# States of a diagonal state-space layer stored by planes of the step index, stepped for all pairs at once, with three early pieces of the gated projection

## The reference

```python
u = (h @ w_in)
lam_bar = jnp.exp(lam * dt)                       # 64 groups x 64 complex states
b_bar = ((lam_bar - 1.0) / lam)[..., None] * b_c
bu = einsum(u, b_bar)                             # 16 inputs of a group -> 64 states
xs[t] = lam_bar * xs[t-1] + bu[t]
y = real(einsum(xs, c_c)) + d_skip * u
g = gelu(y)
val, gate = split(g @ w_glu, 2)
x = x + val * sigmoid(gate)
```

## Time and profile before

| | us |
|---|---|
| median of three runs (lowest, highest) | 950.24 (949.27, 950.56) |
| the profiled execution: its time | 950.29 |
| its span | 948.5 |
| PE busy | 736.2 |
| DVE busy | 302.0 |
| ACT busy | 186.5 |
| POOL busy | 75.1 |

### The profile page before, as it was taken

The page is one execution under the profiler, slowest core; times in us unless marked ns, Lnnn a source line. Parts: engine busy times, 40 slices in busy tenths (PEclk is TensorE's granted clock), DMA queues, the critical chain, the costliest instruction groups (busy, mean ns, idle before and its releaser), DMA issues.

```text
span 948.5 us, 15405 instructions
## 1 busy us (share of the span) xinstructions
PE 736.2 (78%) x6273; PEld 432.3 (46%) x6273; DVE 302.0 (32%) x702; ACT 186.5 (20%) x398; POOL 75.1 (8%) x64
## 2 busy tenths in 40 slices
PE   2969485994697668676699996666398999996696
PEld 1859354432554334343344444333354555553453
DVE  5792997115421001100421533223711111211112
ACT  3653430123110000000300324113210111110012
POOL 6691000002100000000000000001200000000000
PEclk9986797995699888878899997877599999999899
DMA  9520502934399999999990472016089990499991
GB/s 262 148 96 1 179 1 75 419 130 197 103 425 425 424 424 423 424 424 423 390 338 1 178 266 89 0 41 247 1 352 423 420 402 0 158 422 424 422 418 63
DMA packets 58074, 238.40 MB, mean 251 GB/s; under 512 B 17624, under 2 KB 17824, under 8 KB 33440
## 3 DMA queue, kind: packets, MB, share of 16 engines
q1 hardware_dynamic: 56560, 235.25, 62.2%
q0 software_dynamic: 576, 2.10, 0.6%
q10 hardware_dynamic: 880, 0.23, 0.1%
HBM read 236.53 MB, written 1.05 MB: 250 GB/s over the span
## 4 chain that ended last, share of the span: by engine, by line
PE 49%; DVE 19%; SPq 16%; DMA 10%; ACT 3%; issue 2%; ACTq 0%; DVEq 0%
SPq L369 16%; PE ps L1573 9%; PE ps L1504 9%; DMA work<-in_moe_w_down 6%; PE ps L1539 5%; PE ps L1439 4%; PE ps L1486 4%; PE ps L1546 4%; DMA ring<-in_moe_w_down 3%; PE ps L1638 3%; PE ps L1360 1%; PE ps L1295 1%; PE ps L1468 1%; DVE work L961 1%; DVE work L962 1%
## 5 line engine op out<-in xcount | busy, mean ns | idle before, releaser
L1504 PE MATMUL ps<-ring,work 128*32 128x256 f32 x1824 | 148.5, 421 | 34.9 <-DMA ring<-in_moe_w_up 24.0
L1504 PEld LDWEIGHTS ps<-ring,work 128*32 128x32 f32 x1824 | 79.9, 121 | 79.9 <-issue 54.9
L1154 DVE TENSOR_TENSOR work<-ps,work 128x256 f32<-128x256 f32 x21 | 12.9, 616 | 300.4 <-PE ps L1504 300.4
L1504 PE MATMUL ps<-work 128*32 128x256 f32 x864 | 87.1, 425 | 27.5 <-DMA ring<-in_moe_w_up 10.8
L1546 PE MATMUL ps<-work 128*128 128x512 f32 x168 | 77.7, 605 | 0.0
L1486 PE MATMUL ps<-work,hT 128*128 128x128 bf16 x736 | 71.2, 227 | 6.7 <-DVE work L1104 6.7
L1504 PEld LDWEIGHTS ps<-work 128*32 128x32 f32 x864 | 45.5, 122 | 62.7 <-issue 44.3
L1573 PE MATMUL ps<-ring,hT 128*128 128x512 f32 x160 | 70.4, 593 | 0.0
L1539 PE MATMUL ps<-ring,work 128*32 128x512 f32 x496 | 65.5, 595 | 6.1 <-DMA work<-in_moe_w_down 4.4
L1486 PE MATMUL ps<-work 128*128 128x128 bf16 x368 | 68.3, 227 | 0.0
L1486 PEld LDWEIGHTS ps<-work,hT 128*128 128x128 bf16 x736 | 59.6, 102 | 15.8 <-issue 8.6
(11 more groups left out here) (288 smaller groups left out, 990.0 us busy)
## 6 DMA issues: line engine op xcount, KB each, us to landing
ring<-in_moe_w_gate SPq DMA_DIRECT2D x24, 2048.0 KB, 25.3
ring<-in_moe_w_down SPq DMA_DIRECT2D x23, 2048.0 KB, 15.4
ring<-in_moe_w_up SPq DMA_DIRECT2D x17, 2048.0 KB, 23.1
work<-in_moe_w_up SPq DMA_DIRECT2D x15, 2048.0 KB, 22.9
work<-in_moe_w_down SPq DMA_DIRECT2D x9, 2048.0 KB, 27.6
work<-in_moe_w_gate SPq DMA_DIRECT2D x8, 2048.0 KB, 25.9
ring<-in_attn_w_qkv SPq DMA_DIRECT2D x5, 2048.0 KB, 21.2
ring<-in_ssm_w_glu SPq DMA_DIRECT2D x4, 2048.0 KB, 8.8
```

Of the source, the lines that this page charges most:

```text
L1154: TTo(hid.rearrange("s (k p) -> s p k", k=2), ps[:, 7, 0:256].rearrange("s (p k) -> s p k", k=2), sil.rearrange("s (p k) -> s p k", k=2), ...
L1504: ins = mm(ps[s, 6 + j // 2, 0:256], xg[:, k, s], pairs[slots[e // 2]][:, e % 2, k, :], start=(k == 0), stop=(k == KD - 1))
```

## The change

1. `X` is laid out by planes of the step: per partition `i`, `l`, `r`, `h`, with `h` innermost and `r` next. `U4` and `gT` follow the same order of the blocks.
2. `local_states` and `carries` run once for all 32 pairs instead of twice for 16. `skips(0)` and `skips(1)` stand inside `local_states`, after steps 4 and 6.
3. `carried(o)` no longer puts its last sum into `X` but into a copy `Xs[o]` in the order that `y` reads, split by `i`; two small copies bring the plane `l` = 0.
4. `weights(2)`, `weights(3)` and `stack` stand ahead of `powers(mu, ...)`. After the powers DVE keeps the increments of octets 0 and 1 (`inputs_kept`); ACT keeps those of octets 2 and 3 only.
5. PE: `drive(2)` stands ahead of `turn_w1(3, 1)`, and `taps(0)`, `taps(1)` ahead of `drive(3)`. The taps use PSUM banks 6 and 7, and `local_states` waits for the last of octet 3.
6. PE: `glu(2, range(4))` is a third piece ahead of `y(2)`. The outputs come in the order 0, 2, 1, 3.
7. Start: DVE clears a third of what POOL cleared of `W2`, POOL clears the rest only after the normalised input is written, and the exponential on ACT no longer waits for the load of `ssm_d`.
8. SP: the first two expert units wait for `y_done` instead of `state`, the next pair but one for the third GLU output.

```diff
-        X = part(12288, 64 * M).rearrange("p (i r m) -> p i r m", i=2, r=PAIRS)
+        X = part(12288, 64 * M).rearrange("p (i l r h) -> p i l r h", i=2, l=SEG, r=PAIRS)
...
+        GLU_OUT = (4, 6, 0, 4)
+        GLU_ORDER = (0, 2, 1, 3)
...
+        def inputs_kept(copy, o, b):
+
+            src = ps[:, 2 * (o % 2) + b, :].rearrange("p (r i l h) -> p i l r h", r=4, i=2, l=SEG)
+            pr = slice(OCT * o + 4 * b, OCT * o + 4 * b + 4)
+            for i in range(2):
+                copy(X[:, i, 0, pr, 1:SEG], src[:, i, SEG - 1, :, 0:SEG - 1])
+                ins = copy(X[:, i, 1:SEG, pr, :], src[:, i, 0:SEG - 1, :, :])
+            return ins
...
-            clear(part(4096, 8192), 8)
+            pool.wait_ge(normed, 2)
+            clear(part(8192, 4096), 4)
...
-            act.wait_ge(s_lam, 64)
+            act.wait_ge(s_lam, 48)
...
+                    n = SEG if l < SEG - 1 else SEG - 1
+                    dst = X[:, :, l + 1, :, :] if l < SEG - 1 else X[:, :, 0, :, 1:SEG]
+                    by = lambda i: spread(spread(mu[:, i, 0, :], 1, 2), 3, n)
+                    advance(dst, X[:, :, l, :, 0:n], tmp[0][:, :, :, 0:n], tmp[1][:, :, :, 0:n], by)
+                    if l in (4, 6):
+                        skips(l // 2 - 2)
...
+                for i in range(2):
+                    dve.tensor_copy(Xs[o][:, i, :, 0:SEG], X[:, i, 0, pr, :])
+                link(TTo(dst, dst, tmp[0].rearrange("p i l r h -> p i l (r h)"), ALU.add))
+                for i in range(2):
+                    ins = TTo(Xs[o][:, i, :, SEG:64].rearrange("p r (l h) -> p l r h", h=SEG), X[:, i, 1:SEG, pr, :], tmp[1][:, i], ALU.add)
...
-                act.copy(gT[:, 2 * o:2 * o + 2, :].rearrange("p c (m s) -> p c s m", s=SB),
-                         ps[:, o, :].rearrange("p (s c m) -> p c s m", s=SB, c=2)).then_inc(g_ready, 1)
+                for c in range(2):
+                    ins = act.copy(gT[:, 2 * o + c, :].rearrange("p (h l s) -> p s l h", h=SEG, s=SB),
+                                   ps[:, o, :].rearrange("p (s c l h) -> p c s l h", s=SB, c=2, l=SEG)[:, c])
```

More of the change, by code:

```diff
@@ L176, in build @@
         Cb = pre[:, 8192:10240].rearrange("p (i r c) -> p i r c", i=2, r=PAIRS)
+        Xs = [pre[:, 6144 + 1024 * n:7168 + 1024 * n].rearrange("p (i r m) -> p i r m", i=2, r=OCT) for n in range(PAIRS // OCT)]
         t1 = pre[:, 10240:10752]
@@ L387, in _ @@
             sp.wait_ge(w2_ready, 4)
-            sp.wait_ge(state, 4)
+            sp.wait_ge(y_done, 4)
             whole(0, 0, 0)
@@ L673, in _ @@
             keep_g(3)
[L675 to L679, removed]
+            for turn_no, n in enumerate(GLU_ORDER):
+                act.wait_ge(glu_done, turn_no + 1)
+                if turn_no >= 1:
+                    act.wait_ge(mixed, turn_no)
+                act.activation(sig[:, 0, :], ps[:, GLU_OUT[n] + 1, :], ACT.Sigmoid).then_inc(sig_ready, 1)
             def moe(l):
@@ L832, in _ @@
             dve.sem_inc(hid_ready, 1)
+            for k in range(4):
+                ins = dve.memset(part(4096 + 1024 * k, 1024), 0.0)
+            ins.then_inc(half_clear, 1)
             L = lambda n: lam[:, n, :]
@@ L944, in _ @@
             weights(1)
+            weights(2)
+            weights(3)
+            dve.wait_ge(u_done, 8)
+            for n in range(8):
+                stack(dve.tensor_copy, 3, n).then_inc(u4_ready, 1)
             link(dve.tensor_copy(mu[:, 0:2, 0, :], Pw[:, 0:2, 4, :]))
@@ L949, in _ @@
             link(TS(mu[:, 2, :, :], mu[:, 1, :, :], -1.0, None, ALU.mult))
[L950 to L954, removed]
+            for o in range(2):
+                for b in range(2):
+                    dve.wait_ge(v_done, 2 * o + b + 1)
+                    link(inputs_kept(dve.tensor_copy, o, b))
+                    dve.sem_inc(v_kept_x, 1)
             def advance(dst, src, P_, Q_, by):
@@ L962, in advance, with skips @@
                 link(TTo(dst, dst, Q_, ALU.add))
[L964 to L969, removed]
+            def skips(half):
+                dve.wait_ge(k_done, 2 * half + 2)
+                taps = ps[:, 6 + half, :].rearrange("p (q n) -> p q n", q=KD // 2)[:, :, 0:PC]
+                TTo(taps, taps, skip[:, 4 * half:4 * half + 4, :], ALU.add).then_inc(k_ready, 1)
@@ L1397, in _ @@
             turn_w1(3, 0)
+            drive(2)
             turn_w1(3, 1)
-            drive(2)
+            taps(0)
+            taps(1)
             drive(3)
-            for o in range(4):
-                taps(o)
+            taps(2)
+            taps(3)
             def y(o):
```

108 lines of the change are left out of this document (50 added, 58 removed).

## The result

The changed kernel takes 938.39 us (median of 4 runs, 935.32 to 940.88) against 949.75 for the kernel before in the same comparison (949.13 to 950.56): a ratio of 0.9878, 95% interval 0.9845 to 0.9912. Repeated with five rounds it is 939.01 against 948.73, 0.9889 (0.9875 to 0.9904).

The account below looks back on a forecast made before the run. The end of the state-space layer was taken to bound the rest, with PE the bound from `state` 1. With start, input stage and states summed, the GLU's end moved from 207.7 to 202.6: 950.29 - 5.1 = 945.1 us, range 939.5 to 950.5.

Parts of the forecast that it names:

- (d): Output stage: PE is the bound from `state` 1; the last GLU product's end moves from 207.7 to 202.6, -5.1 us.
- third piece: Third early GLU piece ahead of `y(2)`: alone worth nothing, it only moves 6.9 us of PE work.
- (a): Start: the root of the norm moves from 13.60 to about 11.7, -1.9 us for all that follows.
- (b): Input stage: powers behind stacking, drives 0 and 1 take 7.3 us instead of 13.9; states start at 91.5 against 89.91.
- rival A: Input stage: the clock does not fall before `drive(2)`; 5.5 us less, 939.6 us; chance 0.18.
- (c): States: 2.83 us a step, DVE in all 45.9 us against 70; `state` 4 at 137.4, where it was 160.
- Rival C: States: operands repeated along the innermost axis keep 2 ns; 7.8 us on `state` 1, hence 952.9 us; chance 0.12.
- Behind the GLU: Rest of the span behind the state-space layer: a shift of that layer's end moves it one to one.

Follow-up runs that it names:

- third piece undone: Changed kernel with the third early GLU piece put back behind `y(2)` and `y(3)`: 938.29 us, ratio 0.9895 to the kernel before.
- order alone: Kernel before with one edit, DVE's powers moved behind `weights(2)`, `weights(3)` and the stacking: 941.89 us, ratio 0.9882.
- filler: Changed kernel plus three products of 512 columns, result unread, between `turn_w1(3, 0)` and `drive(2)`: 940.32 us, ratio 0.9916 to the kernel before.
- late halves: Changed kernel, states in two halves of 16 pairs, the first still waiting until all octets are kept: 933.3 us, ratio 0.9821 to the kernel before.
- powers first: Changed kernel with DVE's powers back between `weights(1)` and `weights(2)`: 950.0 us, ratio 1.0015 to the kernel before.
- early halves: Changed kernel, states in two halves of 16 pairs, the first starting once DVE has kept octets 0 and 1: 915.14 us, ratio 0.9646 to the kernel before.

## Why the prediction fell short

**The step that failed** is the pricing of PE's work by its pace in one launch. The sum took stretches as they had run in one launch of the kernel before, partly at half clock, and carried them to places where PE comes from other work. In (d) `y(2)` and `y(3)` stood at 9.4 us and took 8.0 in each launch below. The first product of the input stage, whose pace had no term at all, was left at its 5.85 us and took 3.69 to 5.27; 29 matmuls of `y(0)` were taken at 5.49 and took 4.48 to 5.66; and the stretch behind the GLU was taken to keep its length, but was up to 2.9 us shorter. Nearly all of these errors have one sign. The forecast against three profiled launches, of which the third differs only in the place of the third piece (us):

| | forecast | changed kernel | repeated run | third piece undone |
|---|---|---|---|---|
| first product of the input stage | 5.85 | 3.69 | 5.27 | 3.69 |
| first drive | 61.6 | 59.55 | 60.51 | 59.16 |
| states start | 91.5 | 84.48 | 90.11 | 88.45 |
| first GLU product | 135.2 | 127.02 | 133.63 | 130.58 |
| last GLU product ends | 202.6 | 193.0 | 199.6 | 196.5 |
| rest of the span | 740.8 | 740.5 | 737.9 | 740.0 |
| span | 943.3 | 933.5 | 937.5 | 936.5 |

In the repeated run the forecast's span is 5.8 us too long: 1.4 at the start of the states, 0.2 up to the GLU, 1.4 in `y(2)` and `y(3)`, 2.9 behind the GLU. In the changed kernel's first launch it is 9.8: 7.0, 1.2, 1.4 and 0.3. What is the same in all is the 1.4.

**(a) Start, −1.9: right.** The root of the norm ran at 12.15 and 11.15 us in the two launches of the changed kernel, behind its table load as forecast, and at 13.60 before. From ACT's small exponential to the scaling of the input it is 4.76 us in both, against 6.98 before: that is what DVE gains without POOL's clearing beside it. The wait for `ssm_d` shows no gain of its own: the exponential, now released by the load of `log_dt`, ran at 7.90 and 6.91, against 7.48 before. The scaling starts 1.8 and 2.8 us earlier (12.66 and 11.67 against 14.46), and the 1.0 between them is the landing of that load. What the term left out is the product behind it, before, in the changed kernel and in the repeated run:

```profile
21.81 5.85 PE L1316 MATMUL ps<-hT,ring 128*128 128x256 f32 x16 [1.25 <-ACT hT L567]
```

```profile
19.66 3.69 PE L1338 MATMUL ps<-hT,ring 128*128 128x256 f32 x16 [1.25 <-ACT hT L583]
```

```profile
19.00 5.27 PE L1338 MATMUL ps<-hT,ring 128*128 128x256 f32 x16 [1.25 <-ACT hT L583]
```

The same product differs by up to 2.2 us, and with it the launch with the later scaling has the earlier first drive (59.55 against 60.51). The 5.85 us look like work at half clock: a weight load of this product takes 337 ns at the median before. But the windows list a granted clock of 1.00 there in all three launches, so the reason is not shown.

What POOL's clearing costs one DVE operation varies: 0.62 to 0.93 us for those with one tensor input before, 5.90 for one in order alone, and 3.12 for one in the repeated run, which ended at 20.35, as the clearing beside it did (20.28):

```profile
17.23 3.12 DVE L888 TENSOR_SCALAR work<-work 32x128 f32<-32x128 f32 x1
```

The Trainium skill (SBUF — State Buffer, "Who interferes with whom") says that `tensor_scalar` can run in a two-port mode, which takes the port pair that it shares with GpSimd, and then the one fully blocks while the other has it. The traces agree for the kind of operation: 0.62 to 5.90 beside the clearing and 0.21 without it, against 0.27 to 0.28 for nearly all with two tensor inputs in the same stretch. The clearing consists of pieces below 1 us, so 5.90 and 3.12 mean that DVE lost more than one turn; why, no run shows.

**(b) Input stage: the steps right, the reason for the clock wrong.** `weights(2)` straight after `weights(1)`, drives 0 and 1 at full clock (7.33), a wait of PE for DVE's kept banks (4.42 us, forecast 4.1), `drive(2)` at half clock (6.68, forecast 7.0) and the full clock again in the taps: the run with the third piece undone shows all of it. In the five launches in which drives 0 and 1 took 7.33 and no filler stands behind them, the wait was 3.82 to 4.86 and `drive(2)` took 6.68 to 7.06.

The prediction put the fall of the clock down to the idle time. The filler took most of that away (1.81 us left) and `drive(2)` ran at half clock all the same. In three launches (changed kernel, repeated run and late halves) the clock fell inside drives 0 and 1, with PE busy, and in order alone it fell between transposes and drives that lie 1.57 us apart. So an idle time is at most a part of the reason, and the bounds that the prediction set it, 3.3 us kept and 5.30 lost, do not hold. What decides it, no run shows.

For the sum it mattered little: drives that take 11.4 instead of 7.33 use up the 4.4 us in which PE would wait for DVE. In the changed kernel's first launch `drive(2)` and the transposes behind it ran at full clock, and the states start at 84.5 instead of 90.1, 4.7 of the 5.6 us behind the first drive. That is near the 5.5 of rival A, but not its mechanism: the clock did fall, earlier, and was back in time.

**(c) States: right.** 2.85 us a step (2.83), 31.8 to state 1 (31.6), 4.9 for a carried octet (4.8), the keeping 0.8 a bank (0.9). Rival C is refuted by the row at 84.48 and by the run with the steps innermost.

**(d) PE is the bound from state 1: right, with one term too large.** The 9.4 us for `y(2)` and `y(3)` are close to their stretch before (154.12 to 163.66), which began behind a wait of 8.28 us and at half clock. But here, by the prediction's own argument, they follow the GLU without a wait, and they run at full clock (1.00 in 154.4 to 162.4, repeated run). The third piece is worth nothing, as said.

**Behind the GLU.** The prediction let a shift of the GLU's end move the rest of the span one to one. The router's product, before and in the repeated run (PE's timeline):

```profile
219.43 5.95 PE L1468 MATMUL ps<-hT,wr 128*36 128x256 f32 x16 [0.77 <-ACT hT L550]
```

```profile
211.09 3.61 PE L1493 MATMUL ps<-hT,wr 128*36 128x256 f32 x16 [0.77 <-ACT hT L566]
```

It begins at half clock before and runs at full clock here, and from it to the first expert product it is 30.3 us instead of 32.6: 2.3 of the 2.9 us; the rest was not traced. In the changed kernel's first launch it took 32.5 and in the third launch 32.2, and powers first, whose time is that of the kernel before, has the product at 3.62. So this is no property of the change; it differs from launch to launch.

Part of the distance between forecast and median is the base: the profiled launch of before (950.29) lay 0.5 and 1.5 us above the medians of the kernel before in the two comparisons (949.75 and 948.73).

**Was the change a good one?** The forecast asked where DVE's gain ends, and found PE. It did not ask what else ends there: once PE is the bound from state 1 on, the moment of state 1 is all that counts, and stepping all pairs at once delays exactly that, for a saving on DVE that nobody waits for. The order on DVE alone gives 8 to 11 us, about the gain of the whole (the first figure is the difference of the medians, the second that of the ratio); that planes, one run, the new wait and the start roughly cancel follows from the single edits (17 and 2 us for, 6 and 18 against) and was not run as one kernel.

**Open:** why the clock falls inside the drives in one launch, behind them in another and ahead of them in a third; what the two launches of order alone at 932 and 935 us did differently, beyond their higher mean clock; and whether ACT's filling of `Fw`, now ahead of `y(0)` in the early halves, can be moved.

## What to carry to other kernels

When an engine becomes the bound from some point on, price every edit by when it delivers the *first* piece to that engine, not by what it saves in total: one run over all pairs lost 23 us here to the same work cut in two, whose first half could start and be handed on early. When a change has several parts, ask of each whether it alone would do; five moved lines were worth about as much as all eight parts. And when a stretch of TensorE is priced from a row, look at what came before it there and what will come before it here: `y(2)` and `y(3)` were 1.4 us too long for that reason alone.

## What the runs showed of the hardware

- A DVE `tensor_scalar` of 32x128 float32 took 0.21 us alone, 0.62 to 0.93 beside POOL's clearing, and in two launches 3.12 and 5.90, each ending within 0.1 us of the clearing; nearly all operations with two tensor inputs stayed at 0.28 there. Where POOL reads (forming `W2`), about half of DVE's products in the powers took 1.03 to 1.36 instead of 0.18 to 0.29.
- In three launches the granted clock fell from 1.00 to 0.50 during the drives, with PE busy all the time. Drives that began at half clock ran 13.88 us without its coming back; in the transposes and taps behind them it came back.
- A float32 product of 512 on DVE with an innermost stride of 32 bytes takes 1.07 us, contiguous 0.69, a repeated operand in either.
- Single launches of one kernel differed by up to 12 us (order alone, 931.88 to 943.97), and one product of 16 matmuls behind the GLU took 3.61 to 6.11 us by the clock it found.
